# Two transformer blocks on one core: the sums of the norms with tokens on partitions, a reciprocal of 128x4 numbers spread by matmuls, one merged vector tile, and modulation products in later units of attention

## The reference, cut to what matters

```python
def rms_norm(x, g, eps=NORM_EPS):
    xf = x.astype(jnp.float32)
    y = xf * lax.rsqrt(jnp.mean(xf * xf, axis=-1, keepdims=True) + eps)
    return (y * g.astype(jnp.float32)).astype(x.dtype)

def first_block(...):
    h = rms_norm(x, norm1_g[l]);  proj = h @ w_in[l]
    ...
    yb = fox_group(q, k, v, fl, ...)             # ends in rms_norm(o, norm_g)
    x = x + (y @ w_out[l])
    x = x + hier_moe(rms_norm(x, norm2_g[l]), ...)

def second_block(...):
    c_act = jax.nn.silu(c)
    for l in range(DEPTH_2):
        mod = c_act @ w_ada[l] + b_ada[l]        # 6 x 1024 numbers: shifts, scales, gates
        sh1, sc1, gt1, sh2, sc2, gt2 = [m[:, None, :] for m in jnp.split(mod, N_MOD, axis=-1)]
        h = rms_norm_2(x, norm1[l]) * (1.0 + sc1) + sh1
        ...
        x = x + gt1 * (merged @ w_out[l])
        h2 = rms_norm_2(x, norm2[l]) * (1.0 + sc2) + sh2
        hidden = jnp.square(jax.nn.relu(h2 @ w_ff1[l]))
        x = x + gt2 * (hidden @ w_ff2[l])
    return rms_norm_2(x, final_norm)
```

## Time and profile before

| | |
|---|---|
| median of three runs | 3017.85 us (3015.26, 3017.85, 3018.03) |
| profiled execution | 3016.9 us |
| its span in the trace | 3015.1 us |
| busy: PE | 2795.9 us (93%) |
| busy: PEld / DVE / ACT / POOL | 75% / 50% / 36% / 30% |
| DMA | 373.97 MB, mean 124 GB/s |

### The profile page before, as it was taken

How to read it: one execution, slowest core, us unless ns; L and a number is a source line. 1 busy time by engine, 2 the same in 40 slices (tenths; PEclk the granted TensorE clock), 3 DMA queues, 4 the chain that set the end, 5 groups by cost and what they waited for, 6 DMA issues and landing times.

```text
span 3015.1 us, 34366 instructions
## 1 busy us (share of the span) xinstructions
PE 2795.9 (93%) x13302; PEld 2275.9 (75%) x13302; DVE 1519.2 (50%) x1691; ACT 1093.9 (36%) x1229; POOL 894.5 (30%) x196
## 2 busy tenths in 40 slices
PE   7867798899998999999899999889999998999998
PEld 5666565787777888887677888678988877778886
DVE  4633657769973431144237666634311351476666
ACT  3311434367763244233333222233432333332222
POOL 3100110100003234434333444332344343344443
PEclk9789989889999999999999999999999999999999
DMA  4000133659952222222233344322232222334443
GB/s 146 28 0 21 42 111 100 256 201 363 362 196 89 70 70 93 96 86 103 84 119 146 147 181 160 137 70 71 70 105 97 85 92 94 107 147 159 170 158 126
DMA packets 64341, 373.97 MB, mean 124 GB/s; under 512 B 7392, under 2 KB 8416, under 8 KB 28896
## 3 DMA queue, kind: packets, MB, share of 16 engines
q1 hardware_dynamic: 62064, 365.95, 33.7%
q10 hardware_dynamic: 2160, 6.42, 0.6%
HBM read 370.24 MB, written 2.10 MB: 123 GB/s over the span
## 4 chain that ended last, share of the span: by engine, by line
PE 74%; issue 3%; DVE 3%; POOL 1%; ACT 1%; ACTq 0%; DVEq 0%; POOLq 0%
PE pd L239 18%; PE pd L241 18%; PE pd L240 18%; PE pd L255 2%; PE pd L256 2%; PE pd L254 2%; PE pd L1418 2%; PE pd L1420 2%; PE pd L1419 2%; POOL sb_w_lo L217 1%; PE pd L1445 1%; PE pd L1447 1%; PE pd L1446 1%; PE pd L1376 1%; PE px L1571 0%
## 5 line engine op out<-in xcount | busy, mean ns | idle before, releaser
L217 POOL TENSOR_TENSOR sb_w_lo<-sb_raw,sb_w_hi 128x2048 fp32r<-128x2048 f32 x189 | 889.2, 4705 | 2046.5 <-ACT sb_w_hi L208 2046.5
L239 PE MATMUL pd<-sb_h_hi,sb_w_hi 128*128 128x512 f32 x1696 | 678.8, 400 | 44.6 <-DVE sb_h_lo L332 25.6
L240 PE MATMUL pd<-sb_h_lo,sb_w_hi 128*128 128x512 f32 x1696 | 667.8, 394 | 0.0
L241 PE MATMUL pd<-sb_h_hi,sb_w_lo 128*128 128x512 f32 x1696 | 667.3, 393 | 0.0
L208 ACT CAST sb_w_hi<-sb_raw 128x2048 fp32r<-128x2048 f32 x189 | 360.8, 1909 | 331.0 <-PE pd L241 326.9
L239 PEld LDWEIGHTS pd<-sb_h_hi,sb_w_hi 128*128 128x128 f32 x1696 | 322.9, 190 | 124.7 <-DVE sb_h_lo L332 29.7
L239 PE MATMUL pd<-sb_y_hi,sb_w_hi 128*128 128x512 f32 x960 | 382.0, 398 | 27.1 <-issue 17.0
L240 PE MATMUL pd<-sb_y_lo,sb_w_hi 128*128 128x512 f32 x960 | 380.9, 397 | 0.0
L241 PE MATMUL pd<-sb_y_hi,sb_w_lo 128*128 128x512 f32 x960 | 380.9, 397 | 0.0
L240 PEld LDWEIGHTS pd<-sb_h_lo,sb_w_hi 128*128 128x128 f32 x1696 | 323.2, 191 | 69.5 <-issue 2.7
L241 PEld LDWEIGHTS pd<-sb_h_hi,sb_w_lo 128*128 128x128 f32 x1696 | 322.7, 190 | 69.4
(11 more groups left out here) (487 smaller groups left out, 3775.7 us busy)
## 6 DMA issues: line engine op xcount, KB each, us to landing
sb_raw<-in_slabs SPq DMA_DIRECT2D x189, 1024.0 KB, 4.8
sb_V<-in_ada SPq DMA_DIRECT2D x64, 512.0 KB, 6.0
sb_V<-in_moe SPq DMA_DIRECT2D x28, 1024.0 KB, 5.4
sb_QK<-in_moe SPq DMA_DIRECT2D x28, 1024.0 KB, 5.7
sb_raw<-in_moe SPq DMA_DIRECT2D x28, 1024.0 KB, 5.6
sb_ada_early<-in_ada SPq DMA_DIRECT2D x48, 512.0 KB, 4.4
sb_QK<-in_ada SPq DMA_DIRECT2D x32, 512.0 KB, 6.8
sb_xT<-in_x SPq DMA_DIRECT2D x4, 512.0 KB, 5.5
```

Source lines behind the costliest of these rows:

```text
L217: pool.tensor_tensor(w_lo[j][:], raw[j][:], w_hi[j][:].bitcast(F32), ALU.subtract).then_inc(w_lo_ready[j], 1)
L239: pe.matmul(out, w_hi[j][:, cols], hi[:, k], start=(k == 0), stop=False)
L240: pe.matmul(out, w_hi[j][:, cols], lo[:, k], start=False, stop=False)
L241: last = pe.matmul(out, w_lo[j][:, cols], hi[:, k], start=False, stop=(k == KT - 1))
```

## The change

- The sums of the norms: each 128x128 block of squares is now the stationary operand and one column of ones streams, so a block's 128 tokens come out on 128 partitions, as one column of px[0] (token_sums). A tile of 512 tokens takes four matmuls of 128x1.
- The root and the reciprocal go over these 128x4 numbers (norm_root_of, inverse_root). Four matmuls then spread the inverse over all partitions: column b, broadcast to 128x128, against the identity gives block b of 128x512 in px[3] (spread_inverse; px[1] for attention's norm). PE waits for the inverse, DVE for the spread, and the products read PSUM in place of T.
- vec and vec_tail become one tile of 512 columns, 2048 B.
- The identity, now needed by norm 0, is loaded ahead of vec and the first slabs; the start of PE, DVE and of ACT's later part waits for three transfers instead of two.
- The 28 early modulation dots stand in units 4 to 31 instead of 0 to 27.

```diff
@@ -164,9 +164,8 @@
         ones = sb("ones", [P, P])
-        vec = sb("vec", [P, V1_COLS])
-        vec_tail = sb("vec_tail", [P, 512 - V1_COLS])
-        mod = vec_tail[:, 0:ADA_COLS]
+        vec = sb("vec", [P, 512])
+        mod = vec[:, V1_COLS:V1_COLS + ADA_COLS]
         pd = [whole.enter_context(nc.psum_tensor(f"pd{i}", [P, TOK], F32)) for i in range(4)]
...
@@ -262,11 +261,15 @@
                 act.activation(sq[:, 2 * n:2 * n + 2], xT[:, 2 * n:2 * n + 2], ACT.Square).then_inc(norm_sq, 1)
+        def norm_root_of(act, u):
+
+            act.wait_ge(norm_sum, u + 1)
+            act.activation(T[:, 0, 0:TB], px[0][:, 0:TB], ACT.Sqrt, bias=EPS, scale=1.0 / D).then_inc(norm_root, 1)
+
         def norm_scalar(act, u, sq, shift=None, first=0):
             norm_squares(act, sq, range(first, 4))
-            act.wait_ge(norm_sum, u + 1)
-            act.activation(T[:, 0], px[0][:], ACT.Sqrt, bias=EPS, scale=1.0 / D).then_inc(norm_root, 1)
+            norm_root_of(act, u)
             for k in range(KT):
...
@@ -279,18 +282,35 @@
                 for k in range(2 * n, 2 * n + 2):
-                    last = pe.matmul(px[0][:], ones[:], sq[:, k], start=(k == 0), stop=(k == KT - 1))
+                    last = token_sums(pe, sq[:, k], k == 0, k == KT - 1)
             last.then_inc(norm_sum, 1)
+            spread_inverse(pe, u)
+
+        def token_sums(pe, tile, first, final):
+
+            for b in range(TB):
+                last = pe.matmul(px[0][:, b:b + 1], tile[:, b * P:(b + 1) * P], ones[:, 0:1],
+                                 start=(first and b == 0), stop=final, skip_group_check=True)
+            return last
+
+        def spread_inverse(pe, u):
+
+            pe.wait_ge(norm_inv, u + 1)
+            for b in range(TB):
+                last = pe.matmul(px[3][:, b * P:(b + 1) * P], T[:, 1, b:b + 1].to_broadcast([P, P]), ident[:],
+                                 start=True, stop=True)
+            last.then_inc(norm_spread, 1)
         def norm_tail(pe, u, sq, added):
             pe.wait_ge(norm_added, added)
             for k in (0, 1):
-                pe.matmul(px[0][:], ones[:], sq[:, k], start=(k == 0), stop=False)
+                token_sums(pe, sq[:, k], k == 0, False)
             pe.wait_ge(norm_sq, 4 * u + 4)
             for k in (6, 7):
-                last = pe.matmul(px[0][:], ones[:], sq[:, k], start=False, stop=(k == 7))
+                last = token_sums(pe, sq[:, k], False, k == 7)
             last.then_inc(norm_sum, 1)
+            spread_inverse(pe, u)
         def norm_add(dve, u, sq, added):
...
@@ -315,12 +335,17 @@
             act.wait_ge(slab_out[1], m + 2)
+        def inverse_root(dve, u):
+
+            dve.wait_ge(norm_root, u + 1)
+            dve.reciprocal(T[:, 1, 0:TB], T[:, 0, 0:TB]).then_inc(norm_inv, 1)
+            dve.wait_ge(norm_spread, u + 1)
+
         def norm_vector(dve, v, u, sq, gain, shift=None):
-            dve.wait_ge(norm_root, u + 1)
-            v(dve.reciprocal(T[:, 1], T[:, 0]))
+            inverse_root(dve, u)
             for step in range(KT + 1):
                 if step < KT:
-                    dve.scalar_tensor_tensor(sq[:, step], xT[:, step], gain(step), T[:, 1], ALU.mult,
+                    dve.scalar_tensor_tensor(sq[:, step], xT[:, step], gain(step), px[3][:], ALU.mult,
                                              ALU.mult).then_inc(norm_val, 1)
...
@@ -446,12 +472,12 @@
             sp.dma_start(ones[:], t["ones"]).then_inc(vec_loaded, 16)
-            sp.dma_start(vec[:], t["vec1"]).then_inc(vec_loaded, 16)
+            sp.dma_start(ident[:], t["ident"]).then_inc(vec_loaded, 16)
+            sp.dma_start(vec[:, 0:V1_COLS], t["vec1"]).then_inc(vec_loaded, 16)
             for j in range(2):
                 sp.dma_start(raw[j][:], t["slabs"][j]).then_inc(raw_loaded[j], 16)
             sp.dma_start(c1[:], t["c1"]).then_inc(c_loaded, 16)
             sp.dma_start(blk[:], t["blk"]).then_inc(c_loaded, 16)
-            sp.dma_start(ident[:], t["ident"]).then_inc(c_loaded, 16)
             with sp.Fori(1, IN1_PAIRS + 1) as m:
...
@@ -707,8 +733,13 @@
                 pe.wait_ge(fox_sq, k + 1)
-                last = pe.matmul(px[0][:], ones[:], sq_att[:, k], start=(k == 0), stop=(k == 3))
+                last = token_sums(pe, sq_att[:, k], k == 0, k == 3)
             last.then_inc(fox_sum, 1)
+            pe.wait_ge(fox_inv, 1)
+            for b in range(TB):
+                last = pe.matmul(px[1][:, b * P:(b + 1) * P], small[:, 48 + b:49 + b].to_broadcast([P, P]), ident[:],
+                                 start=True, stop=True)
+            last.then_inc(fox_spread, 1)
         @block.scalar
...
@@ -898,12 +929,12 @@
             act.wait_ge(fox_sum, 1)
-            act.activation(T[:, 0], px[0][:], ACT.Sqrt, bias=EPS, scale=1.0 / 512).then_inc(fox_root, 1)
+            act.activation(small[:, 44:48], px[0][:, 0:TB], ACT.Sqrt, bias=EPS, scale=1.0 / 512).then_inc(fox_root, 1)
         @block.vector
         def _(dve):
             v = steps["vector"] = Steps(dve, vector_steps)
-            dve.wait_ge(vec_loaded, 32)
+            dve.wait_ge(vec_loaded, 48)
             norm_vector(dve, v, 0, M[:, 0:8], lambda k: v1("norm1", k))
...
@@ -1091,14 +1122,17 @@
                                         small[:, 40 + p % 4:41 + p % 4], None, ALU.mult), sc_prob, p + 1)
-                if n < ADA_EARLY:
-                    if n == 0:
+                first = len(UNITS) - ADA_EARLY
+                if first <= n < len(UNITS):
+                    if n == first:
                         dve.wait_ge(c_row_ready, 1)
-                    ada_dot(dve, n, n % ADA_RING, n // ADA_RING, ada_early, c_row, mod[:, n:n + 1])
+                    tile = n - first
+                    ada_dot(dve, tile, tile % ADA_RING, tile // ADA_RING, ada_early, c_row, mod[:, tile:tile + 1])
             dve.wait_ge(fox_root, 1)
-            v(dve.reciprocal(T[:, 0], T[:, 0]))
+            dve.reciprocal(small[:, 48:52], small[:, 44:48]).then_inc(fox_inv, 1)
+            dve.wait_ge(fox_spread, 1)
             for k in range(4):
-                v(dve.scalar_tensor_tensor(Y[:, 2 + k], o_att[:, k], v1("fox_norm", k), T[:, 0],
+                v(dve.scalar_tensor_tensor(Y[:, 2 + k], o_att[:, k], v1("fox_norm", k), px[1][:],
                                            ALU.mult, ALU.mult), y_fox, k + 1)
...
@@ -2218,10 +2250,9 @@
             u = 2 + 2 * LAYERS
-            dve.wait_ge(norm_root, u + 1)
-            v(dve.reciprocal(T[:, 1], T[:, 0]))
+            inverse_root(dve, u)
             for k in range(KT):
-                dve.scalar_tensor_tensor(O[:, k], xT[:, k], v1("final", k), T[:, 1], ALU.mult,
+                dve.scalar_tensor_tensor(O[:, k], xT[:, k], v1("final", k), px[3][:], ALU.mult,
                                          ALU.mult).then_inc(norm_val, 1)
...
```

More of the change, by code:

```diff
@@ L187, in build @@
         norm_sq, norm_sum, norm_root = sem("norm_sq"), sem("norm_sum"), sem("norm_root")
-        norm_added = sem("norm_added")
+        norm_added, norm_inv, norm_spread = sem("norm_added"), sem("norm_inv"), sem("norm_spread")
         norm_val, norm_hi, h_ready = sem("norm_val"), sem("norm_hi"), sem("h_ready")
@@ L437, in build @@
             "fox_sq", "fox_sum", "fox_root", "y_fox", "fl_in"))
+        fox_inv, fox_spread = stage_sem("fox_inv"), stage_sem("fox_spread")
         UNITS = [(h, qb) for h in range(8) for qb in range(TB)]
@@ L478, in _ @@
         def _(pe):
-            pe.wait_ge(vec_loaded, 32)
+            pe.wait_ge(vec_loaded, 48)
             norm_tensor(pe, 0, M[:, 0:8])
@@ L492, in _ @@
             pieces(2, 0, 0, 4)
-            pe.wait_ge(c_loaded, 48)
+            pe.wait_ge(c_loaded, 32)
             pe.wait_ge(lora_in, 1)
@@ L720, in _ @@
             norm_scalar(act, 0, M[:, 0:8], first=4)
-            act.wait_ge(vec_loaded, 32)
+            act.wait_ge(vec_loaded, 48)
             act.wait_ge(h_ready, 8)
@@ L949, in _ @@
                 v(dve.tensor_tensor(k_s[:, j], A[:, 2 + j], k_s[:, j], ALU.mult), scaled, j + 1)
-            dve.wait_ge(c_loaded, 48)
+            dve.wait_ge(c_loaded, 32)
             dve.wait_ge(tr_out, 6)
@@ L1625, in _ @@
             norm_squares(act, MG, [3])
-            act.wait_ge(norm_sum, 2)
-            act.activation(T[:, 0], px[0][:], ACT.Sqrt, bias=EPS, scale=1.0 / D).then_inc(norm_root, 1)
+            norm_root_of(act, 1)
             def moe_split(q):
@@ L2276 @@
 DECAY_CHUNK = constants()["decay_chunk"]
-LAYER_VECTOR_STEPS = 52
+LAYER_VECTOR_STEPS = 50
 def lay_out(inputs):
```

## The result

The changed kernel takes 2992.01 us (median of four runs, 2987.03 to 2992.53) against 3016.56 us before (3009.67 to 3018.03, runs of both series together): a ratio of 0.9917, 95% interval 0.9900 to 0.9934. The forecast was 2991. The profiled execution took 2991.93 us with a span of 2990.1, so the two traces differ by 25.0 us, and that is what the table splits. A stage goes from the start of its first matmul to the start of the next stage's first, in either trace.

The account below looks back on a forecast made before the run. PE bounds the kernel, by its own matmul pace and its waits at norms and attention's start. Alignment 22.3, norms 0.4 and attention 3.1 sum to 25.8 us off 3016.9: 2991, range 2972 to 3007.

Parts of the forecast that it names:

- Alignment: Slab and MoE matmuls whose operands start 32 B apart are slow; merging the tiles gains 22.3 us, ends 0 and 24.
- Attention: Start and end of attention: later dots remove VectorE's wait for POOL's copy, gaining 3.1 us, ends +1 and +7.
- worth another 1.1: Start of attention: four dots of 1.23 us less, where PE is late, estimated to gain 1.1 us.
- Norms: Eight norms: narrow sums, shorter root and inverse, and spread together gain 0.4 us, ends -9.4 and +19.8.
- the 0.3 us that the prediction put down for the identity's load: Program start: ident's 64 KB landing ahead of vec delays norm 0's sums by an estimated 0.3 us.
- +0.8, six times 4.8: Norms 1, 3, 4, 5, 6 and FoX (attention's): each gains 0.8 us, 4.8 together, ends -1.8 and +14.4.
- the all-half end: Norm 3 and those priced like it: entirely at half clock, 6.3 us against 6.04, a loss of 0.3.
- What follows each norm, the first slabs at half clock, I leave as it is: First slabs behind each norm: their half clock was taken as unchanged, with no term in the sum.
- Behind its wait for the inverse PE has only slabs ... queued: PE's queue at the norms: the slabs (after norm 1 the routing) behind the inverse wait for the products anyway.
- the offset is not the cause: Rival on alignment: y slabs differ from h slabs in more than the address; 3013.4 us, chance 0.13.
- the clock holds through the narrow sums: Rival on the norms: narrow sums stay at full clock, norms give 19.8 instead of 0.4; 2971.7 us, chance 0.09.
- the kernel gets slower: Rival: narrow sums lower the clock in every norm, y's pace stays; norms -9.4, attention +1, 3025.3 us, chance 0.07.

Follow-up runs that it names:

- run 1: Kernel before with one edit, vec and vec_tail merged into one tile of 512 columns: 2994.37 us, ratio 0.9923 to the kernel before.
- run 2: Changed kernel with an unused 32 B tile behind vec, shifting Y and all behind it back: 3010.51 us, ratio 0.9983 to the kernel before.
- run 3: Not the network: 15 stretches of 96 matmuls of 128x512 differing only in the operands' starts; 226.7 to 233.5 ns a step.
- run 5: Changed kernel with the 28 modulation dots back in units 0 to 27: 2991.77 us.
- run 4: Changed kernel with the old norms (wide sums, root and reciprocal on 128x512), merged tile and later dots kept: 2990.09 us, ratio 0.9917 to the kernel before.
- run 6: Run 4 plus wide matmuls with unread results (fillers) behind each norm's sums: 2991.36 us.
- run 8: Changed kernel with ScalarE's cast of the second slab moved ahead of the last square (norm 0: root), norms 0, 2 to 5: 2978.17 us, ratio 0.9876 to before.
- run 7: Changed kernel with wide throwaway matmuls (fillers) around the narrow sums and behind the spreads: 2994.40 us.
- run 10: Changed kernel with narrow norms, fillers around most sums and spreads, and the second-slab casts moved ahead: 2964.89 us, ratio 0.9836 to the kernel before.

## Why the prediction was right, point by point

- **Alignment** (22.3): measured 22.4 by stages (19.6 in the stages with y slabs for 19.5, 2.8 in MoE for 2.8), and runs 1 and 2 bring it alone and take it away again. The price of a y slab matmul, 6.8 ns, is the 1.30 us by which 192 of them differ between the two traces. The reading that a pair is slow when its operands differ, whichever is off, is what run 3 shows.
- **Attention** (+3.1): 2.7 in the trace. Two of the three parts came as put: +3.1 at the start for the forecast's 3.0, since the product waits for POOL's remainder and no longer for the copy, and -0.8 for -1.0 at the last unit, for the dot ahead of its inverse. The third, "worth another 1.1" for four dots less, is mis-sized: it is +0.4, all of it within 1.2 us behind unit 0's product, and from there to the last units the two traces keep the same distance to 0.1 us, so the four dots less gave nothing there. In the median the term is not resolved (run 5).
- **Norms** (+0.4): -1.9. The mechanism was right: 0.213 a record in norm 0 and in the second half of norms 1, 3, 4 and 5 (norm 6's took 2.13 us, mostly at full), spreads of 2.07 us against 2.1. Norm 0 lost 3.0 and not 3.8, since its sums started at 9.40 and not at 10.2: the 0.3 us that the prediction put down for the identity's load no run shows, with starts between 9.1 and 10.3 in the old order of loads and between 9.3 and 9.9 in the new (without fillers ahead). The mis-sized term is "+0.8, six times 4.8": norms 1, 3, 4, 5, 6 and attention's gave +2.7 together. Norms 3 and 5 came out at the all-half end (-0.1 each), and attention's norm below it: its 32 records ran almost wholly at half, 6.21 us at a mean clock of 0.57, where the wide sums of before stood at 1.00. The step that priced it like norm 3 left out what runs ahead of the sums: attention's last matmuls are narrow too, which I take for the reason without a run that tests it. Norm 2 lost 1.5, not 0.6.
- **What was luck** in the sum: the 1.7 us between norm 0 and attention. Most of it, 1.5 us, is a dozen slab matmuls between two small products, which ran at half in the trace of before and at full in that of after, with nothing of the change near them. The same stretch takes between 394.8 and 398.7 us in the traces of runs 1, 2, 4 and 5, which have no edit in it either. The windows, of before and then of after:

```profile
81.70:85.00 3.30, 3.30 (x9) 2.58 (x8) 2.43 (x1) 1.92 (x4) 3.30 (x1) 0.50 0.02 5
```

```profile
84.20:87.00 2.80, 2.80 (x12) 2.06 (x12) 1.48 (x1) 2.38 (x4) 2.80 (x1) 1.00 0.01 3
```

  With this the total of 25.0 stands beside 25.8; without it the forecast would have been 2.5 too far.
- **The step that failed without showing in the time** is "What follows each norm, the first slabs at half clock, I leave as it is". It came true, and for another reason than I had: that half clock cost nothing, because the second slab's weights ended last (runs 6 and 8). The same goes for "Behind its wait for the inverse PE has only slabs ... queued": the slabs were looked at, their weights on ScalarE's queue were not.
- **Rivals**: that the offset is not the cause fell with runs 1 to 3. That the clock holds through the narrow sums fell for this kernel (0.50 in all of norm 3's second half); in runs 7 and 10 it holds for the sums of norm 3, but only with other work put around them. That the kernel gets slower fell with the alignment, and its loss in the norms, 9.4, was not reached either.

## What to carry to other kernels

Compare the pace of equal matmuls between stages before looking at waits: a few per cent between two operands' starts, unseen in any wait, was 22.4 of the 25.0 us and cost one declaration. When a stop is shortened or a slow clock cured and the time stays, follow the next tile's weights back through every queue they pass; here a cast behind eight others, on an engine that was two thirds idle, held the gain of both. Small work is not cheap where it leaves an engine's clock low: in this kernel most of the narrow sums cost 0.213 us a record, about twice the 0.115 of full clock.

## What the runs showed of the hardware

- fp32r matmuls of 128x128 on 128x512 with a new stationary each take 226.7 ns a step where the starts of the two operands differ by 0, 256, 512 or 1024 B (227.0 with both 32 B on), 231.7 where they differ by 16 B, 229.0 by 64 B and 233.2 to 233.5 by 32, 96 or 128 B (run 3, one execution), at a granted clock of 1.00.
- At the start of the program the granted clock in these traces is not to be relied on. The window of norm 0's sums in the changed kernel shows 1.00, while its records are 0.213 us apart, the pace of half clock elsewhere:

```profile
9.40:23.20 13.80, 13.80 (x64) 13.72 (x64) 0.00 (x0) 3.34 (x3) 4.52 (x1) 1.00 0.73 293
```

- In norm 3 the first 16 records of 128x1, right behind wide slabs, took 1.84 us with and without fillers, 0.115 a record. The second 16 took 1.95 us with two wide records between the halves (run 10) and 3.57 without, at a granted clock of 0.50.
